# A decoder layer with expert retrieval on one core: dense products for the last 32 first keys on the U side too, eight U blocks ahead of the first V pick, and closer rankings

## What is computed

```python
q = (h @ w_query).reshape(B, S, 8, 2, 128)
s = einsum('bshcd,hckd->bshck', q, sub_keys)          # 128 first keys, 128 second keys, per head
top_s, top_i = lax.top_k(s, 16)
cand = top_s[..., 0, :, None] + top_s[..., 1, None, :]
best_s, best_i = lax.top_k(cand.reshape(B, S, 8, 256), 16)
eid = i1 * 128 + i2                                   # one of 16384 experts
g = softmax(best_s)
a = gelu(einsum('td,thkd->thk', hx, expert_u[e]))
return einsum('thk,thkd->td', gw * a, expert_v[e])
```

## Time and profile before

| | |
|---|---|
| three runs, median (lowest to highest) | 1733.74 us (1732.56 to 1734.15) |
| the profiled execution, its own time | 1734.55 us |
| its span in the trace | 1732.8 us |
| busy: PE / DVE / ACT / POOL | 1363.6 / 1339.1 / 654.9 / 957.2 us |
| moved by DMA | 615.55 MB |
| PE's granted clock, mean | 0.877 |

### The profile page before, as it was taken

One profiled execution on the slowest core, in us unless ns is written; L12 is line 12 of the kernel. 1 busy time (PEld: TensorE's weight loads), 2 busy tenths in 40 slices (PEclk: granted clock), 3 DMA queues, 4 the chain that ended last, 5 costly groups with the idle time before them and its releaser, 6 DMA issues.

```text
span 1732.8 us, 19532 instructions
## 1 busy us (share of the span) xinstructions
PE 1363.6 (79%) x7442; PEld 1083.8 (63%) x7442; DVE 1339.1 (77%) x1907; ACT 654.9 (38%) x911; POOL 957.2 (55%) x591
## 2 busy tenths in 40 slices
PE   9999999999979913655555555577767799999976
PEld 8988999988668803554544455576667744444432
DVE  6666656666797999777757878887867877788898
ACT  5665456564201213344444544445557611000000
POOL 3210000000364677887787676788888455767782
PEclk9999999999989956677777787788888789999998
DMA  9876443466699999999999999999999999999997
GB/s 323 286 260 219 122 147 122 132 202 250 263 382 420 387 424 426 406 424 425 425 426 423 413 419 418 423 411 419 423 423 425 368 423 377 414 406 416 413 427 297
DMA packets 159390, 615.55 MB, mean 355 GB/s; under 512 B 20915, under 2 KB 74255, under 8 KB 96703
## 3 DMA queue, kind: packets, MB, share of 16 engines
q0 software_dynamic: 79232, 485.32, 68.2%
q1 hardware_dynamic: 80064, 128.99, 20.7%
HBM read 683.42 MB, written 2.10 MB: 396 GB/s over the span
## 4 chain that ended last, share of the span: by engine, by line
PE 28%; DMA 28%; POOL 17%; DVE 13%; issue 9%; ACT 3%; DVEq 2%; SPq 0%; POOLq 0%; ACTq 0%
DMA v_slot<-in_expert_v_dram,eid 22%; PE psum_all L596 14%; POOL u_slot L532 8%; POOL v_slot L551 7%; DVE u_slot L1825 7%; DMA u_slot<-in_expert_u_dram,eid 5%; PE psum_all L736 4%; PE psum_all L998 2%; POOL v_slot L554 2%; ACT v_slot L1321 1%; PE psum_all L761 1%; PE psum_all L717 1%; DVE xh L1861 1%; PE psum_all L623 1%; PE psum_all L621 1%
## 5 line engine op out<-in xcount | busy, mean ns | idle before, releaser
L1825 DVE SCALAR_TENSOR_TENSOR u_slot<-u_slot,xh 128x2048 f32<-128x2048 f32 x256 | 578.3, 2288 | 132.6 <-DMA u_slot<-in_expert_u_dram,eid 130.6
L998 PE MATMUL psum_all<-ident,v_slot 128*128 128x128 f32 x2304 | 389.5, 341 | 289.1 <-ACT v_slot L1321 288.9
L532 POOL DMA_INDIRECT u_slot<-in_expert_u_dram,eid x256 | 437.9, 1711 | 288.6 <-DVE u_slot L1825 116.0
L998 PEld LDWEIGHTS psum_all<-ident,v_slot 128*128 128x128 f32 x2304 | 350.7, 179 | 324.1 <-ACT v_slot L1321 319.8
L551 POOL DMA_INDIRECT v_slot<-in_expert_v_dram,eid x224 | 419.3, 1872 | 119.1 <-issue 65.1
L1321 ACT ACTIVATE v_slot<-v_slot,gate 128x2048 f32<-128x2048 f32 x144 | 287.4, 2000 | 319.8 <-DMA v_slot<-in_expert_v_dram,eid 319.6
L1861 DVE SCALAR_TENSOR_TENSOR xh<-v_slot,gate,xh 128x2048 f32<-128x2048 f32 x100 | 235.1, 2351 | 52.8 <-DMA v_slot<-in_expert_v_dram,eid 46.4
L1443 DVE TENSOR_TENSOR w_lo<-w_ring,w_hi 128x512 fp32r<-128x512 f32 x240 | 156.5, 687 | 79.9 <-ACT w_hi L1049 76.8
L596 PE MATMUL psum_all<-act_hi,w_hi 128*128 128x256 f32 x640 | 184.6, 289 | 1.1 <-DVE w_lo L1443 1.0
L596 PE MATMUL psum_all<-act_hi,w_lo 128*128 128x256 f32 x640 | 180.7, 282 | 0.0
L596 PE MATMUL psum_all<-act_lo,w_hi 128*128 128x256 f32 x640 | 180.6, 282 | 0.0
(11 more groups left out here) (296 smaller groups left out, 1688.0 us busy)
## 6 DMA issues: line engine op xcount, KB each, us to landing
w_ring<-in_w_in_dram SPq DMA_DIRECT2D x88, 512.0 KB, 4.8
u_slot<-in_expert_v_dram SPq DMA_DIRECT2D x40, 1024.0 KB, 8.7
wo_ring<-in_w_out_dram SPq DMA_DIRECT2D x32, 512.0 KB, 5.2
wq_ring<-in_w_query_dram SPq DMA_DIRECT2D x32, 512.0 KB, 10.4
w_ring<-in_cmp_k_w_dram POOLq DMA_DIRECT2D x16, 512.0 KB, 5.5
w_ring<-in_cmp_v_w_dram POOLq DMA_DIRECT2D x16, 512.0 KB, 4.2
u_slot<-in_expert_u_dram,eid POOLq DMA_INDIRECT x256, 19.6
v_slot<-in_expert_v_dram,eid POOLq DMA_INDIRECT x256, 18.6
```

Source lines behind the costliest of these rows:

```text
L532: nc.gpsimd.indirect_dma_start(out=u_slot[m % RU][:, :], out_offset=None, in_=expert_u[0], in_offset=bass.IndirectOffsetOnAxis(ap=eid[:, n ...
L998: ins = nc.tensor.matmul(bank[(4 if n < PH else 0) + c // 4][:, P * (c % 4):P * (c % 4) + P], v_slot[m % RV][:, P * c:P * c + P], ident[:, ...
L1825: V.scalar_tensor_tensor(u_slot[m % RU][:, :], u_slot[m % RU][:, :], 1.0, xh[:, n // PH, :], ALU.mult, ALU.mult, accum_out=u_dot[:, n, k:k ...
```

## The change

- **Both sides are dense for the same 32 first keys.** `FD` goes from 40 to 32. All 256 U gathers and all 256 V gathers leave out the rows of these keys.
- **The dense U product.** SP loads 32 blocks of 128 U rows (1 MB each) through two slots of their own (`x_slot`). A block has four quarters j: TensorE transposes four 128x128 pieces (`u_transposes`), ScalarE copies them from PSUM (`u_out`), TensorE multiplies them with h of all 256 tokens (`u_dots`), and behind the fourth quarter ScalarE applies gelu to the 128x256 sums (`u_gelu`). TensorE works one quarter behind its transposes. Ahead of it h is transposed once more (`h_transposes`, `h_out`).
- **Where it stands.** The first 32 quarters (`X_FIRST`, eight blocks) are ahead of the first V pick on TensorE and ScalarE; each of the other 96 is ahead of one of V picks 0 to 95.
- **The dense matrices** now hold the softmax weight (`weights_of`), and `weigh` on VectorE multiplies them with the gelu sums as it takes them out of PSUM; `dense_out` on ScalarE is gone. `hot_rows(0, b)` moves to 5 dots for 4 b from dot 198, `dense_rows(0, b)` to V picks 112 to 127.
- **Rankings** 2 to 7 stand behind dots 17, 24, 32, 39, 47 and 54 (before: behind 17, 33, 49, 65, 81 and 97), rankings 8 to 15 behind dots 64 to 130 (before 113 to 177).
- **Slots:** U 8 to 6 (and the two of the blocks), V 7 to 6. SP asks for two quarters of the second query matrix earlier.

```diff
-RU = 8
-RV = 7
+RU = 6
+RX = 2
+RV = 6
-FD = 40
+FD = 32
+X_FIRST = 32
-IDS_AT.update({(n, 1): n + 1 for n in range(1, 9)})
+IDS_AT = {(0, 4): 1, **{divmod(17 + 15 * (n - 2) // 2 if n < PH else 64 + 19 * (n - PH) // 2, TOPK): n for n in range(2, NU)}}
-HOT0_AT = {178 + 5 * b // 2: b for b in range(NG_T)}
+HOT0_AT = {198 + 5 * b // 4: b for b in range(NG_T)}
...
+        sp.wait_ge(S["wq_used"], 12)
+        sp.wait_ge(S["t1_mm"], 4)
+        for i in range(FD):
+            if i >= RX:
+                sp.wait_ge(S["ut_mm"], 4 * (i - RX + 1))
+            first = ROWS + NKEY * XORD[i]
+            sp.dma_start(x_slot[i % RX][:, :], expert_u[0][first:first + NKEY, :]).then_inc(s_xu[i % RX], 16)
...
             nc.gpsimd.indirect_dma_start(out=u_slot[m % RU][:, :], out_offset=None, in_=expert_u[0],
-                                         in_offset=bass.IndirectOffsetOnAxis(ap=eid[:, n, k:k + 1], axis=0)
-                                         ).then_inc(s_u[m % RU], 16)
+                                         in_offset=bass.IndirectOffsetOnAxis(ap=eid[:, n, k:k + 1], axis=0),
+                                         bounds_check=ROWS - 1, oob_is_err=False).then_inc(s_u[m % RU], 16)
...
+        def u_transposes(j):
+            i, g = divmod(j, 4)
+            if g == 0:
+                pe.wait_ge(s_xu[i % RX], 16 * (i // RX + 1))
+            if j >= 2:
+                pe.wait_ge(S["ut_ok"], j - 1)
+            for c in range(4):
+                ins = nc.tensor.transpose(bank[j % 2][:, P * c:P * c + P],
+                                          x_slot[i % RX][:, 512 * g + P * c:512 * g + P * c + P], ident[:, :])
+            ins.then_inc(S["ut_mm"], 1)
+        def u_dots(j):
+            i, g = divmod(j, 4)
+            pe.wait_ge(S["ut_ok"], j + 1)
+            if g == 0 and i:
+                pe.wait_ge(S["xa_ok"], i)
+            for c in range(4):
+                ins = nc.tensor.matmul(bank[2][:, 0:SEQ], uT[:, j % 2, c, :], hT2[:, 4 * g + c, :],
+                                       start=(g == 0 and c == 0), stop=(g == 3 and c == 3))
+            if g == 3:
+                ins.then_inc(S["xs_mm"], 1)
+        def u_step(j):
+            if j < 4 * FD:
+                u_transposes(j)
+            if 0 < j <= 4 * FD:
+                u_dots(j - 1)
...
+        for j in range(X_FIRST):
+            u_step(j)
         for m in range(PE_PICKS):
             n, k = divmod(m, TOPK)
+            u_step(X_FIRST + m)
...
+        def u_out(j):
+            act.wait_ge(S["ut_mm"], j + 1)
+            nc.scalar.activation(uT[:, j % 2, :, :], bview(j % 2, 4, P), ACT.Copy).then_inc(S["ut_ok"], 1)
+        def u_gelu(i):
+            act.wait_ge(S["xs_mm"], i + 1)
+            if i in XIDS:
+                act.wait_ge(S["ids_ok"], XIDS[i])
+            nc.scalar.activation(wst[:, XORD[i], :, :].rearrange("p a t -> p (a t)"), bank[2][:, 0:SEQ], ACT.Gelu_apprx_tanh
+                                 ).then_inc(S["xa_ok"], 1)
...
         for m in range(PE_PICKS):
             if m in UNIT_AT:
                 unit(UNIT_AT[m])
...
+            u_step(X_FIRST + m)
...
             scaled(m)
...
+        def weigh(t, b):
+            g = NG_T * t + b
+            if b == 0:
+                dve.wait_ge(S["xa_ok"], FD)
+            dve.wait_ge(S["dense_mm"], g + 1)
+            cols = wst[:, :, t, G_TOK * b:G_TOK * b + G_TOK]
+            V.tensor_tensor(cols, bview(4 * t + g % 2, G_TOK, FD).rearrange("p t f -> p f t"), cols, ALU.mult
+                            ).then_inc(S["dense_ok"], 1)
```

More of the change, by code:

```diff
@@ L1394, in unit, with u_step @@
+        def u_gelu(i):
[4 more added lines that the diff above has]
+                                 ).then_inc(S["xa_ok"], 1)
+        def u_step(j):
+            if j < 4 * FD:
+                u_out(j)
+            if j and j % 4 == 0 and j <= 4 * FD:
+                u_gelu(j // 4 - 1)
         def unit(n):
@@ L1398, in _ @@
         act.wait_ge(S["eps2_ok"], 1)
+        for i in range(2 * KC // 4):
+            h_out(i)
+        for j in range(X_FIRST):
+            u_step(j)
         unit(3)
@@ L1402, in _ @@
                 unit(UNIT_AT[m])
-            if m == V0_PICKS + 1:
-                unit(13)
+                if UNIT_AT[m] == 12:
+                    for n in range(13, NU):
+                        expo_gate(n)
+            if m == V0_PICKS + 4:
+                gelu_unit(13)
+            u_step(X_FIRST + m)
+            if m == PICKS0_AT:
+                picks_out(0)
             scaled(m)
-            if m == 80:
-                picks_out(0)
-            if m % 2 and 93 <= m < 93 + 2 * NG_T:
-                dense_out(0, (m - 93) // 2)
             if m == V0_PICKS - 1:
@@ L1413, in _ @@
                 picks_out(1)
-                expo_gate(14)
-                expo_gate(15)
-            if m >= V0_PICKS + 5:
-                build_out(m - V0_PICKS - 5)
-        for b in range(TOPK - 5, NG_T):
-            build_out(b)
-            if b == NG_T - 4:
-                sums_out(1)
-        gelu_unit(15)
+            if m >= BUILD1_AT and (m - BUILD1_AT) % 2 == 0:
+                if m == BUILD1_AT:
+                    act.drain()
+                key_rows(m - BUILD1_AT + 1)
+        for b in range(PE_PICKS - BUILD1_AT, NG_T):
+            if b % 2 == 0:
+                key_rows(b + 1)
+        sums_out(1)
+        for n in (14, 15):
+            gelu_unit(n)
         act.wait_ge(S["coef_ok"], NU)
@@ L1905, in _ @@
                     dve.drain().then_inc(S["h1_ok"], 1)
-                if n and k == (10 if n < NU - 2 else 2):
+                if n and n <= 12 and k == 10:
+                    weights_of(n - 1)
+                if (n, k) == (13, 4):
+                    for u in range(12, NU):
+                        weights_of(u)
+                if n and n < NU - 1 and k == 10:
                     gates_of(n - 1)
@@ L1914, in _ @@
             hot_rows(1, b)
+        for b in (NG_T - 2, NG_T - 1):
+            weigh(1, b)
         V.tensor_scalar(xh[:, 1, :], xh[:, 1, :], ALPHA, None, ALU.mult)
@@ L1918, in _ @@
             if m == PE_PICKS + TOPK:
-                gates_of(NU - 1)
+                for u in (NU - 2, NU - 1):
+                    gates_of(u)
             if m == TOPK * NU - 10:
```

168 lines of the change are left out of this document (89 added, 79 removed).

## The result

The changed kernel took 1887.83 us (median of 4 runs, 1883.99 to 1898.1) against 1733.95 (4 runs beside it): 1.0894 times as long, 95% interval 1.0849 to 1.0940. It is slower. The profiled execution took 1886.75 us (span 1885.0), 152.2 us more span than before.

| stretch | before | after | difference | forecast |
|---|---|---|---|---|
| to the first scaling of a V row | 664 | 726 | +62 | +46 |
| V picks 0 to 95 | 464 | 528 | +64 | +131 |
| V picks 96 to 143 | 248 | 258 | +10 | -10 |
| after the last scaling | 357 | 373 | +16 | -20 |

A forecast was written before the change was run, and what follows sets the result against it. The DMA was taken to bound the kernel before; the change makes the first 96 picks a TensorE-ScalarE chain. Cycle +131, start +46, picks 96 to 143 -10, tail -20: +147 on 1734.55 gives 1882 us, range 1790 to 1975.

The forecast's parts named there:

- four signs: First scaling at 700 to 730; scalings 0 to 95 5.7 to 6.7 us each; 96 to 143 in 220 to 248; tail 330 to 347.
- the second: Picks 0 to 95: 5.7 to 6.7 us each, ScalarE and TensorE waiting for each other, hardly for DMA; about 330 GB/s.
- signs of being wrong: Scalings running ahead of copies, clock leaving 0.75 to 0.95, or transposes and products costing otherwise than the like shapes.
- The cycle of picks 0 to 95: Pick, next quarter's transposes (T), copy and scaling one behind another: 6.2 us a pick instead of 4.83, +131 us.
- a mean of 0.82: TensorE's granted clock in picks 0 to 95, taken from an earlier stage: 36% of time at half clock, 5.33 to 6.2 us.
- rival that went by the rule, 2024 us: Clock low throughout the picks, since transposes do not lift it: 7.68 us a pick, 2024 us in all; chance 9%.
- products D: TensorE's four matmuls of a U quarter with h: 0.89 us at the high clock, hidden except on each fourth pick.
- The start: Before V pick 0: later rankings, h evacuations and eight U blocks move the first scaling from 664 to 712 us, +46.
- Picks 96 to 143: Fewer bytes a pick, but the first build on 16 consecutive picks at 5.3 us: 237 against 248 us, -10.
- The tail: After 1376 us: 123 MB instead of 134, gain bounded by VectorE's 46 us of waits: -20 us (-10 to -27).
- rival DMA-bound as before: Whole kernel still held by the DMA, so 34 MB less show in full: 81 us faster, 1654 us; chance 6%.
- late loads of U (1918): U blocks land late ahead of the first pick: +82 for +46, clock as forecast, 1918 us; chance 9%.

The follow-up runs named there:

- Run 1: Changed kernel with TensorE one quarter block further ahead, transposes for ScalarE's next copy before the V pick instead of behind it: 1838.07 us, ratio 1.0598 to the kernel before.
- Runs 2 to 4: Changed kernel with one of four U products a quarter: alone 1942.98 us; with 11 identity transposes added 1886.38 us; with three unused products added 1891.09 us.
- run 2: Changed kernel with one matmul instead of four in each quarter of the dense U product (products incomplete): 1942.98 us, ratio 1.1185 to the kernel before.
- run 3: Changed kernel with one of four products a quarter and 11 identity transposes into an unused bank behind each: 1886.38 us, ratio 1.0886 to the kernel before.
- run 7: Changed kernel with the first token tile's dense build spread over every second pick from 97 to 127, instead of each from 112: 1858.31 us, ratio 1.0698.
- run 8: Changed kernel with TensorE one quarter block further ahead and the first build spread over every second pick from 97: 1801.57 us, ratio 1.0385 to the kernel before.
- Run 11: Kernel before with its last 112 V gathers bounded to the first 128 rows, nearly all those rows left out: 1713.25 us, ratio 0.9880.
- run 10: Kernel before with U gathers from the ninth on bounded to the first 128 rows, nearly all U rows left out: 1657.47 us, ratio 0.9554.
- run 9: Kernel before with U gathers from the ninth on checked, leaving out rows of the 40 dense keys: 1676.05 us, ratio 0.9675.

## Why the prediction was right, and where its terms were not

1882 was said and 1888 measured, for the reason given: the order (copy behind transposes behind pick behind scaling) takes the picks off the DMA and makes them a chain. Run 1 shows it by undoing the order alone. But that the total came within 6 us is luck: three terms fell short by 16, 20 and 36 us and one was 67 us too high.

Of its four signs only the first came as a number, the first scaling at 726 us. The waits of the second came too, but with 5.5 us a pick and 366 GB/s instead of 5.7 to 6.7 and 330; picks 96 to 143 (258 us) and the tail (373) lie outside theirs. Two of the things that it called signs of being wrong did happen: the clock left 0.75 to 0.95 (0.96), and the products cost twice what the like shape was read to cost.

- **The cycle of picks 0 to 95.** The sum at the high clock was 5.33 us; the trace has 4.98, with 6.49 on every fourth pick: 5.36. Pick and T together (2.40 us for 2.46), copy (0.60) and gelu (0.39 for 0.38) came as estimated. The step that failed is "a mean of 0.82": it was 0.96, and the picks 5.5 us, not 6.2. I took the clock from the nearest stage of before and did not ask how much busier TensorE gets. It is at work for 407 of 520 us (78%) here, against 264 of 464 (57%) in the picks before. Runs 2 to 4 show that this work holds the clock: 0.77 without three of four products, 0.96 with them or with as many microseconds of transposes. I had argued the other way round, from TensorE's gap in each cycle. The price of the low clock was about right: run 2's rows have 3.45 + 0.82 = 4.27 us for pick and T, at a mean of 0.77, where 4.59 was worked out for the low level alone.
- **Transposes and the clock.** The granted clock was 0.96 in run 3, where TensorE has 31 transposes and one product in a pick. The Trainium skill ("TensorE: Matmul & The Clock Gate", Part 4: PE-mode transpose) says that they do not count as busy in the way other matmuls do. This case disagrees for f32 transposes: 11 of them beside the pick's 20 did for the clock what three products did (0.96 both; 1886 and 1891 us). The rival that went by the rule, 2024 us, did not come.
- **The products D.** Said to be 0.89 us for four, hidden. The row has 1.89 us for x8: a product of 256 columns in f32 is two records of about 0.24 us each, and the page has L1023 x1024 for 512 products. The query row's x64 are 32 matmuls in the same way (the page before has L761 x640 for 320). In three picks of four this was covered all the same (TensorE still waits 0.85 us for the scaling); in each fourth it is the 1.13 us that the gelu waits. At the start it was not covered.
- **The start.** +62 for +46. Chain, and late rankings as said: the last scores are out at 644.2 us (forecast 643), h at 652.3 (652). What failed is the block of 5.5 us that then waits for its load. TensorE itself is the bound: 2.17 us a quarter, 9.0 us a block, and the loads are hidden behind it:

```profile
659.88 0.60 PE L1012 MATMUL psum_all<-ident,x_slot 128*128 128x128 f32 x4
...
660.32 1.89 PE L1023 MATMUL psum_all<-hT,uT 128*128 128x256 f32 x8
...
662.04 0.60 PE L1012 MATMUL psum_all<-ident,x_slot 128*128 128x128 f32 x4
```

  It is D's size again; run 2, with a quarter of D, began its picks 18 us earlier. The term's own sums slip by a few us as well: 712 less 664 is 48, not 46, and its bounds come to +38 and +80 by their working, not +30 and +82.
- **Picks 96 to 143.** -10 was said, +10 came. I had the build on 16 consecutive picks as 5.3 us of VectorE's work each. It is a second chain: VectorE may not make the next one-hots until TensorE's matmuls with the last but one are done, and those stand behind the picks. The row L1927 above shows 40.6 us of that wait, in a stretch in which POOL also waits 42.5 us for VectorE's dots. Spreading the build took out 29.5 us of the total (run 7) and 36.5 (run 8). The prediction's 0.49 us for 320 elements is a row of VectorE's one-hots in the trace before (L1854, 0.49 us), and not among; the weighing itself came as estimated, 0.42 us.
- **The tail.** -20 was said, +16 came. What failed is that fewer bytes would bring the adds down to POOL's 2.47 us. They stand as far apart as before, 2.93 us for 2.89: 100 of them start within 290.4 us after and 286.3 before, at 2.35 us each, and VectorE waits 48.3 us for rows, where it had waited 46.4.

```profile
L1952 DVE SCALAR_TENSOR_TENSOR xh<-v_slot,gate,xh x100: 2344/2352/2354, 1553.6 to 1844.0; 128x2048 f32<-128x2048 f32 x100
```

  They start 42 us behind the end of the last scaling, in the kernel before 35 (1368.7 to 1403.9): VectorE is further behind with its dots. That is 7 of the +9 by the scalings, the adds' spacing 4, the end -2; the other 7 are those of the cut. Less than before is moved in 1560 to 1840 us, 376 GB/s, but at a share of 0.97. Run 11 shows that the adds would go faster with the rows gone. Why the DMA's share stays near 1 at 8% fewer bytes a second is not settled. The 40 slices of 1560 to 1840 us, 7 us each, show it most plainly in their last third:

```profile
DMA  9999999999999999999999999998989989999988
GB/s 423 423 401 385 384 403 392 421 386 335 401 399 414 420 412 391 412 398 404 416 417 400 394 417 425 428 366 330 317 296 321 317 316 337 328 321 337 342 311 291
```

- **The bytes.** Said: 34 MB less; measured 35.8 (615.55 to 579.72). The rival DMA-bound as before, with 1654 us, went by all of them at 420 GB/s. Even without the chain it could not have come: run 1 is behind the DMA and takes 1838, since the start and the build have prices of their own, and run 10 shows that the kernel before still takes 1657 with nearly all of its U rows gone. The late loads of U (1918) did not occur, nor did the low clock (2024); run 2, with TensorE's work taken away, went that way as far as 1943.
- **The check on POOL.** It was put at 0.16 us a gather, hidden, from the means of 1.71 us (U, unchecked) and 1.87 (V, checked). The trace after does not bear that out: there all U gathers are checked and take 1.67 us on average, the V gathers 1.73.

What stays open: the price in time of a row left out. It was 0.011 us of an engine in the tail of run 11. In 700 to 1100 us the queue took 6451, 6246 and 3520 us of engines for 167.9, 152.8 and 69.9 MB with 6,168, 11,192 and 21,836 small packets (before, run 9, run 10): taking each as so much a moved row and so much a left-out one, I estimate 0.07 us a row left out from before and run 9, 0.04 from before and run 10, so one price does not fit all. Which of VectorE and POOL holds the picks at 4.4 us is open too. Not tried: rankings apart as before with U dense (the dense weights take the scores' place, so they cannot be).

## What to carry to other kernels

When a producer's step is put between two steps of a loop that has been a pipeline, write down for each engine what stands ahead of what, and follow one round: here one quarter block more of lead in TensorE's order was worth 50 of the 154 us. Before taking a stretch's clock from the stretch before, ask how the engine's load changes; on a chain through TensorE, 1.4 us a pick of idle filled or emptied moved a run by 57 us. Count the records of a row against the instructions of the program before dividing its time by them. And before counting bytes as time, look how far below the DMA the next bound lies: here a tenth.

## What the runs showed of the hardware that was not expected

- Taking matmuls away made the kernel slower (1888 to 1943 us), and putting transposes of nothing in their place brought it back (1886): granted clock 0.96, 0.77, 0.96 in the picks.
- An indirect gather makes a packet of every row that its bound leaves out: 79,232 in the queue with 485, 406 and 227 MB (before, run 9, run 10).
- A f32 product with 256 moving columns is two records in the trace, 1.89 us for eight at the high clock; a f32 transpose of 128 columns is one, 1.97 us for sixteen.
